# A two-layer decoder trunk: prologue loads and angles reordered, a fifth shift tile on TensorE, up products by halves, moved row sums, two homes for oa and ob

## The reference

```
c_act = silu(c)
for l in range(2):
    mod = c_act @ ada_w[l] + ada_b[l]          # six vectors of 1024: shift, scale, gate, twice
    h = rmsnorm(x, mix_pre_g) * (1 + sc_m) + sh_m
    t = h @ w_in                                # split into the inputs of three mixers and gate logits
    y_lru = rglru(...) @ lru_wo;  y_ret = retention(...) @ ret_wo;  y_mla = mla(...) @ mla_wo
    merged = sigmoid(g0) * y_lru + sigmoid(g1) * y_ret + sigmoid(g2) * y_mla
    x = x + g_m * rmsnorm(merged @ w_out, mix_post_g)
    h = rmsnorm(x, ffn_pre_g) * (1 + sc_f) + sh_f
    up = causal_dwconv(h @ w_up, conv_w, conv_b)   # width 3, 5632 columns
    x = x + g_f * rmsnorm((gelu(up[g]) * up[u]) @ w_down, ffn_post_g)
```

## Time and profile before

| | us |
|---|---|
| median of 3 runs | 983.22 |
| lowest, highest | 983.09, 984.32 |
| the profiled execution | 986.28 |
| its span, first to last instruction | 984.5 |
| PE busy in the span | 955.5 |
| DVE busy | 718.4 |
| ACT busy | 525.1 |

### The profile page before, as it was taken

One profiled execution on the slowest core, in us unless ns is written; L12 is line 12 of the kernel. 1 busy time (PEld: TensorE's weight loads), 2 busy tenths in 40 slices (PEclk: granted clock), 3 DMA queues, 4 the chain that ended last, 5 costly groups with the idle time before them and its releaser, 6 DMA issues.

```text
span 984.5 us, 17698 instructions
## 1 busy us (share of the span) xinstructions
PE 955.5 (97%) x6976; PEld 888.6 (90%) x6976; DVE 718.4 (73%) x958; ACT 525.1 (53%) x701; POOL 43.6 (4%) x85
## 2 busy tenths in 40 slices
PE   7999999999998999999989999999999999999997
PEld 7889989999987999999969999899999799999996
DVE  4689766676677898786975966676657789676765
ACT  4346855455446655544673485643445656554554
POOL 0000000000000100000000000000000000000000
PEclk7799999999999999999999999999999999999999
DMA  9985755566572786776637864556736557555451
GB/s 352 378 256 184 248 170 165 193 193 215 174 267 87 276 306 238 255 254 231 238 111 213 274 198 167 154 187 211 242 110 236 192 200 270 193 186 178 151 187 44
DMA packets 134141, 206.39 MB, mean 210 GB/s; under 512 B 6336, under 2 KB 104384, under 8 KB 133952
## 3 DMA queue, kind: packets, MB, share of 16 engines
q1 hardware_dynamic: 122416, 162.07, 50.0%
q0 software_dynamic: 11520, 41.95, 11.7%
q10 hardware_dynamic: 144, 1.51, 0.4%
HBM read 204.46 MB, written 1.05 MB: 209 GB/s over the span
## 4 chain that ended last, share of the span: by engine, by line
PE 89%; ACT 3%; DVE 3%; DMA 2%; SPq 1%; issue 1%; DVEq 0%; ACTq 0%
PE banks L1682 79%; DMA raw<-in_w_in 2%; PE banks L1698 1%; DVE w_lo L1091 1%; PE banks L1968 1%; PE banks L1971 1%; SPq L473 1%; PE banks L1706 1%; PE banks L1812 1%; PE banks L1794 1%; DMA raw<-in_ada_rows 1%; ACT w_hi L583 1%; PE banks L1742 1%; ACT h L632 1%; PE banks L1831 1%
## 5 line engine op out<-in xcount | busy, mean ns | idle before, releaser
L1682 PE MATMUL banks<-h_lo,w_hi 128*128 128x256 f32 x1504 | 427.3, 284 | 8.9 <-DVE w_lo L1091 6.0
L1682 PE MATMUL banks<-h_hi,w_lo 128*128 128x256 f32 x1504 | 421.4, 280 | 0.0
L1682 PE MATMUL banks<-h_hi,w_hi 128*128 128x256 f32 x1504 | 421.1, 280 | 0.0
L1682 PEld LDWEIGHTS banks<-h_lo,w_hi 128*128 128x128 f32 x1504 | 284.3, 189 | 13.6 <-DVE w_lo L1091 7.3
L1682 PEld LDWEIGHTS banks<-h_hi,w_lo 128*128 128x128 f32 x1504 | 284.3, 189 | 2.3 <-issue 1.4
L1682 PEld LDWEIGHTS banks<-h_hi,w_hi 128*128 128x128 f32 x1504 | 284.1, 189 | 0.0
L1091 DVE TENSOR_TENSOR w_lo<-raw,w_hi 128x2048 fp32r<-128x2048 f32 x96 | 219.4, 2289 | 68.0 <-ACT w_hi L583 67.7
L583 ACT ACTIVATE w_hi<-raw 128x2048 fp32r<-128x2048 f32 x96 | 182.6, 1912 | 116.3 <-PE banks L1682 95.9
L1597 DVE TENSOR_TENSOR w_lo<-raw,w_hi 128x2048 fp32r<-128x2048 f32 x42 | 96.0, 2285 | 18.3 <-ACT w_hi L960 18.3
L1573 DVE SCALAR_TENSOR_TENSOR EF<-banks,par,EF 128x254 f32<-128x254 f32 (+1 forms) x176 | 76.8, 478 | 43.4 <-ACT EF L941 38.8
L960 ACT ACTIVATE w_hi<-raw 128x2048 fp32r<-128x2048 f32 x42 | 80.4, 1914 | 33.9 <-PE banks L1682 33.9
(11 more groups left out here) (282 smaller groups left out, 1262.0 us busy)
## 6 DMA issues: line engine op xcount, KB each, us to landing
raw<-in_w_in SPq DMA_DIRECT2D x52, 1024.0 KB, 6.0
raw<-in_ffn_w_up SPq DMA_DIRECT2D x44, 1024.0 KB, 5.1
adw<-in_ada_rows POOLq DMA_DIRECT2D x80, 512.0 KB, 4.8
raw<-in_ffn_w_down SPq DMA_DIRECT2D x22, 1024.0 KB, 5.0
raw<-in_w_out SPq DMA_DIRECT2D x8, 1024.0 KB, 6.8
raw<-in_ret_wo SPq DMA_DIRECT2D x4, 1024.0 KB, 5.0
raw<-in_lru_wo SPq DMA_DIRECT2D x4, 1024.0 KB, 6.5
raw<-in_mla_wo SPq DMA_DIRECT2D x4, 1024.0 KB, 6.9
```

What stands on the lines that cost most here:

```text
L1682: ins = MM(ps, lhs, rhs, start=first and n == 0, stop=last and n == 2)
```

## The change

Six edits:

1. The parameter vectors travel in three DMAs: `ada_b` and `mix_pre_g` of layer 0 alone stay at the old place, the rest goes behind block 2 and the positions. ACT issues the tables behind the split of block 3. POOL's first two tile loads wait for the high parts of four blocks and for the five tile products.
2. Tile 12 is multiplied on PE, between the first and second value product of layer 0.
3. The retention angles are computed ahead of the low part of block 3; the row sums of the mixer go behind splits 6 to 12, 14, 16 and 17 and no longer behind 3 and 5.
4. In the merge, step 6 has one sum and step 9 two; in step 7 the sum goes behind the two splits.
5. The first up product waits for each half of h_lo in the order in which it uses them, and ACT's list in `half_end` has the second modulation of the first 128 tokens behind the squares and the first `h_high`.
6. Each of the four tensors of oa and ob is 16 elements longer. The branch outputs start at element 8 (`oa_hi` ...), merged rows and hidden tiles at element 0 (`la_hi` ...). The spacer `space_b` is 7 elements shorter.

```diff
@@ VECTORS, NPAR, first_rows
-    [("tap0", 44), ("tap1", 44), ("mix_pre_g", 8), ("ffn_pre_g", 8), ("mix_post_g", 8), ("ffn_post_g", 8),
+    [("tap0", 44), ("tap1", 44), ("ffn_pre_g", 8), ("mix_post_g", 8), ("ffn_post_g", 8),
-    [("ada_b", 48)],
+    [("ada_b", 48), ("mix_pre_g", 8)],
-NPAR = 2 * P + 48
+NPAR = 2 * P + 56
-    return np.ascontiguousarray(tiles[[0, 1, 4, 5]])
+    return np.ascontiguousarray(tiles[[0, 1, 4, 5, 6]])
@@ tensors
-        sb("space_b", [P, 15])
+        sb("space_b", [P, 8])
-        oa_hi, oa_lo = sb("oa_hi", [P, 4, T], F32R), sb("oa_lo", [P, 4, T], F32R)
-        ob_hi, ob_lo = sb("ob_hi", [P, 5, T], F32R), sb("ob_lo", [P, 5, T], F32R)
+        o_home = [sb(n, [P, k * T + 16], F32R) for n, k in (("oa_hi", 4), ("oa_lo", 4), ("ob_hi", 5), ("ob_lo", 5))]
+        def o_views(start):
+            return [t[:, start:start + k * T].rearrange("p (k t) -> p k t", t=T) for t, k in zip(o_home, (4, 4, 5, 5))]
+        oa_hi, oa_lo, ob_hi, ob_lo = o_views(8)
+        la_hi, la_lo, lb_hi, lb_lo = o_views(0)
-        ON_PE = (0, 2, 8, 10)
+        ON_PE = (0, 2, 8, 10, 12)
@@ hidden_tile, merged_hi, merged_lo, out_proj: la and lb in place of oa and ob
@@ sync
-                    sp.dma_start(par[:], A["vectors"]).then_inc(vec_in, 16)
+                    sp.dma_start(par[:, 0, 2 * P:], A["vectors"][:, 0, 2 * P:]).then_inc(vec_in, 16)
                         sp.dma_start(pos_i, A["positions"][0, :].partition_broadcast(P)).then_inc(pos_in, 16)
+                        sp.dma_start(par[:, 0, 0:2 * P], A["vectors"][:, 0, 0:2 * P]).then_inc(vec_in, 16)
+                        sp.dma_start(par[:, 1, :], A["vectors"][:, 1, :]).then_inc(vec_in, 16)
@@ gpsimd
             pool.wait_ge(ada0_red, ADA0 - len(ON_PE))
+            pool.wait_ge(ada0_used, len(ON_PE))
+            pool.wait_ge(hi_ready.s, hi_ready.at(0, 4))
@@ scalar, half_end
                     modulate(l2, n, 0, 0)
-                    modulate(l2, n, 0, 1)
                     square(l2, n + 1, 1, 0)
                     square(l2, n + 1, 1, 1)
                     h_high(l2, n, 0, 0)
+                    modulate(l2, n, 0, 1)
                     h_high(l2, n, 0, 1)
@@ scalar
             split_block(0, 2)
-            act.dma_start(cst[:, NFIRST:NCONST], consts[:, NFIRST:NCONST]).then_inc(tables_in, 16)
...
                 split_block(l, 3)
+                if l == 0:
+                    act.dma_start(cst[:, NFIRST:NCONST], consts[:, NFIRST:NCONST]).then_inc(tables_in, 16)
+                    act.wait_ge(vec_in, 48)
@@ vector, first_modulation
-                on_pe, on_dve = slice(4 * half, 4 * half + 2), slice(4 * half + 2, 4 * half + 4)
-                dve.wait_ge(ada0_used, 2 * half + 2)
+                tiles = (2, 3)[half]
+                on_pe, on_dve = slice(4 * half, 4 * half + tiles), slice(4 * half + tiles, 4 * half + 4)
+                dve.wait_ge(ada0_used, 3 * half + 2)
-                dve.wait_ge(ada0_red, 6 * half + 6)
+                dve.wait_ge(ada0_red, 5 * half + 6)
@@ vector
-            for n in range(12, ADA0):
+            for n in range(13, ADA0):
-            mixer_sums = {j: n for n, j in enumerate((3, 5, 7, 8, 9, 10, 11, 12, 14, 16))}
+            mixer_sums = {j: n for n, j in enumerate((6, 7, 8, 9, 10, 11, 12, 14, 16, 17))}
-                mixer_split(l, 3)
                 if l == 0:
+                    dve.wait_ge(vec_in, 48)
                     dve.wait_ge(pos_in, 16)
                     step(V.tensor_copy(rs2[:, 0], pos_i))
                     angles(sinr, cosr, inv_ret)
+                mixer_split(l, 3)
@@ vector, merge
-                    ada_sum(l, 10 + m + (m > 4) + (m > 6))
-                    if m in (4, 6):
+                    if m != 7:
+                        ada_sum(l, 10 + m + (m > 4) + (m > 9))
+                    if m in (4, 9):
                         ada_sum(l, 11 + m + (m > 4))
...
+                    if m == 7:
+                        ada_sum(l, 11 + m)
@@ tensor
                 v_product(0, 0)
                 if l == 0:
+                    first_modulation(12)
                     v_product(1, 0)
@@ tensor, up_proj(n, part, slot, j_done, starts=False)
                         for k in range(DK):
+                            if starts and b == 0 and k % 4 == 0:
+                                pe.wait_ge(n_lo.s, n_lo.at(l, 7 + k // 4))
-                pe.wait_ge(n_lo.s, n_lo.at(l, 8))
-                up_proj(0, 0, at_slot(l, NM), RING + NM + 1)
+                up_proj(0, 0, at_slot(l, NM), RING + NM + 1, True)
```

More of the change, by code:

```diff
@@ L375, in hidden_tile @@
         def hidden_tile(i):
-            hi, lo, n = (ob_hi, ob_lo, 0) if i is PAIRS - 1 else (oa_hi, oa_lo, 2) if i is PAIRS - 2 else (oa_hi, oa_lo, 0)
+            hi, lo, n = (lb_hi, lb_lo, 0) if i is PAIRS - 1 else (la_hi, la_lo, 2) if i is PAIRS - 2 else (la_hi, la_lo, 0)
             return [t[:, n:n + 2, :].rearrange("p a b -> p (a b)") for t in (hi, lo)]
@@ L903, in merged_hi @@
                         product_done(act, l, J[("gate", 2, 3)])
-                    A_(flat2(ob_hi if i < 2 else oa_hi, i % 2), flat2(h32, i), ACT.Copy, scale=0.5).then_inc(m_hi.s, 1)
+                    A_(flat2(lb_hi if i < 2 else la_hi, i % 2), flat2(h32, i), ACT.Copy, scale=0.5).then_inc(m_hi.s, 1)
                 for m in range(12):
@@ L1238, in first_modulation @@
                 ks, bias = slice(4 * half, 4 * half + 4), PC(0, "ada_b", 0, 2 * DK)
-                on_pe, on_dve = slice(4 * half, 4 * half + 2), slice(4 * half + 2, 4 * half + 4)
-                dve.wait_ge(ada0_used, 2 * half + 2)
-                V.tensor_tensor(mod[:, on_pe], PS[:, (7, 5)[half], 2 * P:2 * P + 2], bias[:, on_pe], ALU.add)
-                dve.wait_ge(ada0_red, 6 * half + 6)
+                tiles = (2, 3)[half]
+                on_pe, on_dve = slice(4 * half, 4 * half + tiles), slice(4 * half + tiles, 4 * half + 4)
+                dve.wait_ge(ada0_used, 3 * half + 2)
+                V.tensor_tensor(mod[:, on_pe], PS[:, (7, 5)[half], 2 * P:2 * P + tiles], bias[:, on_pe], ALU.add)
+                dve.wait_ge(ada0_red, 5 * half + 6)
                 V.tensor_tensor(mod[:, on_dve], mraw[:, on_dve], bias[:, on_dve], ALU.add)
@@ L1524, in merged_lo @@
                     dve.wait_ge(m_hi.s, m_hi.at(l, i + 1))
-                    hi, lo = (ob_hi, ob_lo) if i < 2 else (oa_hi, oa_lo)
+                    hi, lo = (lb_hi, lb_lo) if i < 2 else (la_hi, la_lo)
                     V.scalar_tensor_tensor(flat2(lo, i % 2), flat2(h32, i), 0.5, flat2(hi, i % 2).bitcast(F32), ALU.mult,
@@ L2105, in _, with up_proj @@
                 pe.wait_ge(mod_ready.s, mod_ready.at(l, 2))
-                def up_proj(n, part, slot, j_done):
+                def up_proj(n, part, slot, j_done, starts=False):
                     pe.wait_ge(lo_ready.s, lo_ready.at(l, j_done))
```

## The result

The changed kernel took 988.95 us (median; 985.29 to 990.24), the kernel before 983.77 us beside it: ratio 1.0049, 95% interval 1.0032 to 1.0066, or about 4.8 us more where 3.6 less were forecast. Its profiled execution took 988.63 us, span 987.0; that of before 986.28, span 984.5. So the two traces differ by 2.5 us and the medians by 5.2; the traces can place only the first.

A forecast was written before the change was run, and what follows sets the result against it. PE, busy 955.5 of a 984.5 us span, was taken as the bound, so savings count only where it waits. Terms -0.9 + 0 + 1.0 - 2.9 - 0.8 = -3.6 us gave 979.6 us, range 975.5 to 984.

The forecast's parts named there:

- Step 4: Merge steps: the second sum in step 9 makes PE wait 0.5 us a layer, +1.0 us for two layers.
- The other half of the step: Merge: moving a sum behind step 7's splits and one from step 6 gains nothing; the 2.00 us wait stays.
- Parts 1 to 3: Prologue: new loads, fifth tile on PE and angles first together move block 4 from 59.21 to 58.3, -0.9 us.
- the 59.2 at which the prediction calls itself wrong: Prologue: the prediction counts itself wrong if block 4 starts after 59.2, against 59.21 before and 58.3 forecast.
- Block 3's early landing: Prologue loads: with tables and ada_w tiles issued later, block 3 lands at 41.1, 6.4 us earlier.
- the high clock under the small products: Prologue, fifth tile: the 16 one-column products run at the high clock and are done at 36.5.
- the low clock rival: Prologue: small products at the low clock, block 4 between 60.1 and 60.8; sum -1.4, 981.8 us; chance 0.27.
- the tables are then late next: hidden: Prologue: tables issued at about 46.4 land until about 59, before the first rotation near 69, so cost nothing.
- Part 5: First up products by halves of h: start moves from 313.75 to 312.3, -1.45 us a layer, -2.9 us.
- Part 6: Homes of oa and ob: 0.8 us gained on 732 moving-operand products, nothing on 720 products of 512 columns.
- the rival in which the address gains: Stationary operands in 720 products of 512 columns: up to 13.7 us back, 966 us, half 973; chance 0.09.

The follow-up runs named there:

- b_merge: The kernel before with the merge order of the fourth edit alone; 988.91 us, 1.0048 of the kernel before.
- b_merge_late: b_merge with step 9's second sum behind its two splits instead of ahead of them; 984.36 us, 1.0004 of the kernel before.
- ho_exp: ho with ACT's exponentials put behind the high part that merge step 9's gate needs; 977.15 us, 0.9918 of the kernel before.
- a_merge_old: The changed kernel with the merge order of before; 982.25 us, 0.998 of the kernel before.
- load_tile: load_exp_sum with the fifth tile on PE; 976.49 us, 0.992 of the kernel before.
- after_late: The changed kernel with merge step 9's second sum behind that step's two splits; 982.63 us, 0.9971 of the kernel before.
- b_tile: The kernel before with the fifth tile on PE alone; 982.5 us, 0.999 of the kernel before.
- angles_tile: angles_best with the fifth tile on PE, loads as before the change; 973.67 us, 0.990 of the kernel before.
- load_tab_tile: load_tab_old with the fifth tile on PE; 974.4 us, 0.9898 of the kernel before.
- b_halves: The kernel before with the up products by halves of h and ACT's new order alone; 983.03 us, 0.998 of the kernel before.
- ho: The kernel before with the halves and the homes (fifth and sixth edits) alone; 982.41 us, 0.9962 of the kernel before.
- b_loads: The kernel before with the new loads, the angles ahead of block 3 and row sums from block 6 alone; 984.08 us, 1.0004 of the kernel before.
- angles_best: ho_exp with the MLP's third sum behind its splits, angles ahead of block 3's split, mixer sums from block 6, old loads; 974.29 us, 0.9896.
- load_exp_sum: ho_exp with the MLP's third sum behind its splits, plus the change's loads and angles, no fifth tile; 977.91 us, 0.9921 of the kernel before.
- load_tab_old: load_exp_sum with the tables issued at their old place, ahead of the first conversions; 971.31 us, 0.987 of the kernel before.
- b_homes: The kernel before with the two homes for oa and ob alone, vectors 8 columns a layer wider; 981.37 us, 0.9971 of the kernel before.
- a_merge_tile_old: a_merge_old with tile 12 back on DVE, so no fifth tile on PE; 980.39 us, 0.9969 of the kernel before.

## Why the prediction was wrong

**Step 4, the merge order, failed.** The prediction priced the second sum in step 9 at its own 1.15 us against 0.7 us of slack: a wait of 0.5 us, +1.0 us for both layers. It asked what stands behind the sum, and not what the sum itself waits for. There are two `adw` buffers, and the tile of step 9's second sum goes into the one that step 8's sum frees. Its load is issued then (267.92) and lands some 3.6 us later, 1.55 us after DVE has come to it. It measured +4.6 us in the trace, +4.7 alone (b_merge), +0.2 with the sum moved behind the splits (b_merge_late), and the whole change is 0.9971 with that one cure. The other half of the step held: the old 2 us wait stayed, and ho_exp shows whose it is.

**Parts 1 to 3, the prologue.** Forecast block 4 at 58.3, measured 60.8, past the 59.2 at which the prediction calls itself wrong. Block 3's early landing and the high clock under the small products came out as worked out. The third value product was at 42.33 for 41.4: the first one started at 30.14 for 29.6, and twelve of them took 5.27 us for 5.1. Two things were missing. The clock fell behind the gap of 1.99 us, which cost 1.6 us (24 products took 7.22 us for 5.6); the low clock rival has the right end, 60.1 to 60.8, by another way: the clock had risen, and fell again. That is not in every trace with the tile, all of which have that gap: the changed kernel, a_merge_old and load_tile have the fall, after_late, b_tile, angles_tile and load_tab_tile not. Nor is it the tile's alone: b_merge, b_halves, ho, b_loads and angles_best fall there without it, behind gaps of 2.03 to 2.69 us. The kernels a_merge_old and after_late have the prologue of the change and start block 4 at 59.0 and 59.5, so part of the 60.8 belongs to this one execution. And "the tables are then late next: hidden" was argued for the rotations that need the tables, not for block 4 beside them: load_exp_sum puts block 4 at 59.7 by its DMA alone, after_late at 59.46. load_tab_tile, which has no such collision and no fall of the clock, starts it at 57.7 with the tile in: there the forecast of 58.3 holds within 0.6 us. In the changed kernel's trace the late products hide the late block: ACT's wait before block 4 is for PE.

**Part 5, halves:** -1.40 us in each layer in the trace and -1.43 alone, for -1.45 forecast. The wait that it bared was not foreseen: DVE is earlier in the MLP, its third sum comes before its tile, and 1.6 us are given back before 811.43. Alone it measured -2.0, not -2.9.

**Part 6, homes:** the size was off, in the good direction. oa and ob lost 1.5 and 1.9 ns of distance each, -1.2 us together, and the 720 products of 512 columns 1.2 ns, -0.9, where nothing was forecast. The sign of the last is that of the rival in which the address gains, at a fifteenth of its size.

**What stays open.** The parts alone add up to +4.7 - 2.0 - 2.8 - 1.0 + 0.4 = -0.7 us, and the whole is +4.8. Without the merge order the whole is -2.0 (a_merge_old) or, cured, -2.9 (after_late), where the other parts add up to -5.4. The tables, whose collision with block 4 each prologue shows differently, and the third sum, which waits for its tile only where halves make DVE early, can be part of that; no run shows how much. The rest lies within uncertainties of some 1.5 us each, or in stretches of low clock: each costs up to 1.7 us and they fall in other places from kernel to kernel. Why is not shown.

## What to carry to other kernels

Before moving an operation that consumes a prefetched buffer, follow the buffer back: which earlier consumer frees it, when is its load then issued, and does load latency fit between the two; if not, place it behind whatever others wait for. A load moved "out of the way" collides with what its new moment releases: look for the stretch in which the DMA engines stand idle and put it there. When several things are late in a prologue, cure one at a time with the others already cured, since the latest of them hides the rest: load_tab_old, with halves, homes, both cures, the new loads and neither tile nor late tables, takes 971.31 us, 0.987 of before.

## What the runs showed of the hardware

The distance of dense products depends on where operands start. Moving operands at 96 bytes past a multiple of 128 gave 119.9 ns for 256 columns, with the high parts moved to 32 bytes it is 118.2 (b_homes, the change), with high and low parts at 32 it is the same (b_loads). h, high and low at 32 bytes too, has 116.9, so the remaining 1.3 ns have another cause, which is open. The Trainium skill (SBUF — State Buffer; Specifications) gives cachelines of 16 bytes, by which all of these starts are alike; the measurement decides.

A gap on PE can cost more than itself. Every trace here has stretches at the 1.2 GHz level after 36 us, each of 3.4 us, or 6.8 us in two cases, and each 3.4 us costs up to 1.7 us. Behind its waits of 1.99 us before 42.33 and 2.06 us before 250.21 the changed kernel has one; behind those of 3.75 and 3.83 us before block 4 load_exp_sum and a_merge_tile_old have the double length. It isn't the gap alone: b_tile and after_late have none behind the same gap near 40 us, and at 111 to 118 and 582 to 593 us many traces have one with no wait of over 0.9 us near it. load_tab_old, which waits under 0.9 us at 40 and 248, has two such stretches after 40 us (112 and 583, beside the one at the very end), the changed kernel four (43, 118, 251, 592).
